# GpSimd adds the final norm's shift in place of VectorE, in the last stage of a decoder layer

## The chip, the cores and the metric

The kernel runs on one core of one Trainium2 chip. Its time is the device time in microseconds (us) of that core. Before the change it is 2271.53 us, the median of 3 runs (2271.29 to 2274.31). The engines are called by the profile's names: PE is TensorE, PEld its weight load, DVE VectorE, ACT ScalarE, POOL GpSimd, and SP the engine that issues DMAs.

## The reference

One layer of a decoder runs for 1024 prompt tokens and 8 sample tokens: attention with three key/value sets, a gated linear recurrence, a merge, a first layer norm, a mixture of 64 experts with a shared expert, and a second layer norm. What matters here is the last line:

```
def layer_norm(x, g, b):
    mu = mean(x); var = mean(square(x - mu))
    return (x - mu) * rsqrt(var + 1e-5) * g + b
...
    ffn = moe(x)                                       # routed + shared experts
    return layer_norm(DN_ALPHA * x + ffn, ln2_g, ln2_b)   # 1024 + 8 rows of 1024
```

The other place that the diff touches is the decode attention over the selected keys: a masked softmax of 8 sample tokens, whose probabilities are scaled, turned by PE and multiplied with the values.

## The kernel before

Each engine runs its own program in order; the engines meet through semaphores. A helper keeps count of them: `E.do(ins, sem)` lets an instruction raise a semaphore (its engine's own chain if none is named), `E.step(ins, sem)` does that and then waits for it on the same engine.

The order of the work is written out by hand. After the attention and the merge comes the expert stage, a loop in which PE multiplies, ACT and DVE take PSUM out, and POOL gathers and scatters rows by indirect DMA. When it is over, SP loads two sets of sums back from memory (L748, L750) into `x1tok` and `other`: nine tiles, eight of 128 tokens and one of the 8 sample tokens, 1024 columns each, float32.

The last stage ("tail") goes tile by tile, m = 0 to 8:

- PE (L1530) adds the two sets of a tile into PSUM, with the identity as weights; there are four PSUM places, so that from the fifth tile on it waits for `normed` of the tile four back. It raises `summed`.
- DVE (L2607 to L2613) waits for `summed` of tile m and takes its statistics: two BATCH_NORM_STATS2 over the halves (L2419, L2420), BATCH_NORM_AGGREGATE (L2421), adding epsilon (L2422). Then it runs `scaled_out(m - 1)` for the tile before: wait for `normed`, multiply by the scale `lnw[:, 2]` (L2601), add the shift `lnw[:, 3]` (L2602), raise `fin_done`. Then it waits for ACT's square root of tile m, takes the reciprocal (L2612) and minus the mean times it (L2613, a SCALAR_TENSOR_TENSOR of 128x1 whose two tensor inputs both lie in SBUF), and raises `mean_done`.
- ACT takes the square root (L1925) and, after `mean_done`, writes the normed tile from PSUM into `x1tok` (L1927), raising `normed`.
- SP (L753 to L755) waits for `fin_done` of each tile and writes it out. At the end it waits for all outputs.
- POOL has nothing in the tail. Its last instructions are those of the expert loop (L2708 to L2713, L2699).

In the decode attention, `dp_ready` counts the steps of DVE's probabilities: PE waits for 4, 5 and 6 before it turns pieces of them, and DVE raises it to 6 at L2215. DVE then copies the turned second half out of PSUM (L2217) and raises `dt_ev2`, for which PE waits at L1200, with `held` (POOL's copies) behind it. Later DVE raises `dp_ready` once for each block of the recurrence (L2278), and ACT waits for 6 + n at L1793.

Of the kernel before, what the change touches and what calls it, by code (L numbers as in the profile page):

```python
# [17 lines left out]
ALU = mybir.AluOpType  # L18
# [9 lines left out]
NT = SEQ // P + 1  # L28
# [161 lines left out]
def build(nc, a, o, x1_dram, y_dram):  # L190
    ctx = ExitStack()
    with ctx:
        arena = ctx.enter_context(nc.sbuf_tensor("arena", [P, 52736], F32))
        PS = ctx.enter_context(nc.psum_tensor("PS", [P, 8, 512], F32))
        names = {}

        def sem(name):
            if name not in names:
                names[name] = ctx.enter_context(nc.semaphore(name))
            return names[name]  # L200
# [4 lines left out]
        def at(off, *shape):  # L205
            n = int(np.prod(shape))
            assert off + n <= 52736, (off, shape)
            v = arena[:, off:off + n]
            if len(shape) == 2:
                v = v.rearrange("p (a b) -> p a b", a=shape[0])  # L210
            elif len(shape) == 3:
                v = v.rearrange("p (a b c) -> p a b c", a=shape[0], b=shape[1])
            return v
# [90 lines left out]
        PTb = at(TMP + 4100, NPG, 64)  # L304
# [40 lines left out]
        def quarter(x, h, j):  # L345
            return x[:, h * HT + j * QT:h * HT + (j + 1) * QT]
# [5 lines left out]
        x1tok = at(12256, NT, D)  # L352
        xr = at(21472, 2, D)
        lnw = at(25568, 4, D)
# [135 lines left out]
        def rows_of(t):  # L490
            return P if t < NT - 1 else BD
# [41 lines left out]
        def targets(i):  # L533

            u1, u0 = ucb[:, 1, 3:3 + NTOK], ucb[:, 0, 3:3 + NTOK]
            if i in (0, 2, 4):
                return u1, u0
            if i in (1, 3, 6):
                a0, b0 = {1: (1, 2), 3: (0, 1), 6: (2, 0)}[i]
                return gg[:, a0, :], gg[:, b0, :]  # L540
            if i == 5:
                return gg[:, 1, :], u1
            if i < YA:
                return mT[:, 2 * (i - YB), :], mT[:, 2 * (i - YB) + 1, :]
            if i < GX:
                return RT[:, 2 * (i - YA), :], RT[:, 2 * (i - YA) + 1, :]
            return sg[:, 0, :], sg[:, 1, :]
# [211 lines left out]
        def _(pe):  # L759
            E = Engine(pe, sem("pe_chain"), met[0], met[1:])  # L760
# [110 lines left out]
            for j in range(NT - 1):  # L871
                t = ORDER[j + 1]
# [140 lines left out]
            def own_values(slot, cols, first):  # L1013

                for b in range(BD):
                    probs = (pself[0:8, 2, :] if slot else sm_self[0:8, :])[:, col[b]:col[b] + 8]
                    ins = pv(b, probs, kvtok(8)[0:BD, cols:cols + P], first=first and b < 4)
                return ins
# [178 lines left out]
            dt_end(turn(PS[0:8, bank, 0:64], pself[0:64, 1, 0:8], 64), "own")  # L1197
            dt_taken("own")
            own_values(1, 384, False)
            pe.wait_ge(sem("dt_ev2"), 1)  # L1200
            pe.wait_ge(sem("held"), 2)
            for h4 in range(2):
                for t in range(NPG):
# [144 lines left out]
            for m in range(1, NT):  # L1348
                t = TAIL[m]
# [172 lines left out]
            for t in range(NT):  # L1522
                m, n = t, rows_of(t)
# [11 lines left out]
        def _(act):  # L1535
            E = Engine(act, sem("act_chain"), met[1], (met[0], met[2]))
            fn = nc.scalar.activation

            def copy(out, in_):
                return fn(out, in_, ACT.Copy)  # L1540
# [53 lines left out]
            for j in range(NT - 1):  # L1594
                m, t = j + 1, ORDER[j + 1]
# [112 lines left out]
            for b in range(1, BD):  # L1708
# [10 lines left out]
                if b == 6:  # L1719
                    n = ct_at["s"]  # L1720
                    act.wait_ge(sem("ct_done"), PC + n + 1)
                    E.do(copy(sm_self[0:8, :], PS[0:8, CT_BANKS[n % 3], 0:64]), sem("ct_a"))
                    n = ct_at["p"]
# [55 lines left out]
            def gelu_of(u):  # L1779

                act.wait_ge(st_cb, ADD * (u + 1))
                g = gg[:, GELU[u], :].rearrange("p h (t j c) -> p h t j c", t=2, j=2)[:, :, :, u % 2, :]
                E.do(fn(g, g, ACT.Gelu_apprx_tanh), sem("g_ev"))

            for i in range(len(PAIRS)):
                d1, d2 = targets(i)
                for j in range(2):
                    u, bank = 2 * i + j, 4 * j
                    n = AFTER.get(u - 1)
                    if n is not None:  # L1790
                        act.wait_ge(sem("r_mm"), n + 1)
                        if n:
                            act.wait_ge(sem("dp_ready"), 6 + n)  # L1793
                        E.do(fn(rr.rearrange("p (a b) -> p a b", a=4), PS[:, bank:bank + 4, 0:QT], ACT.Sigmoid, bias=vec[:, n, 37:38]), sem("r_ev"))
                        act.wait_ge(sem("i_mm"), n + 1)
                        if n:
                            act.wait_ge(sem("hs_done"), n)
                        E.do(fn(ii.rearrange("p (a b) -> p a b", a=4), PS[:, 4 - bank:8 - bank, 0:QT], ACT.Sigmoid, bias=vec[:, n, 38:39]), sem("i_ev"))
                    act.wait_ge(st_mm, PROD * u + 1)
                    if j == 0 and i in (0, 2, 4):  # L1800
                        act.wait_ge(sem("xc_done"), i + 1)
                    if j == 0 and i in (3, 5, 6):
                        act.wait_ge(sem("stg_done"), 2 if i == 3 else 5)
                    if i >= GX and u - 2 * GX >= 2:
                        act.wait_ge(sem("mg_done"), u - 2 * GX - 1)
                    E.do(copy(quarter(d1, 0, j), PS[:, bank, 0:QT]), st_ev)
                    if n is not None:
                        E.step(fn(aa, rr, ACT.Exp, scale=lam[:, 3, n:n + 1]))
                        E.do(fn(RT[:, n, :], aa, ACT.Square))
                        E.do(fn(rr, rr, ACT.Tanh, scale=lam[:, 4, n:n + 1]), sem("a_done"))  # L1810
                    act.wait_ge(st_mm, PROD * u + 2)
                    if i == 5 and j == 0:
                        act.wait_ge(sem("xc_done"), 6)
                    E.do(copy(quarter(d2, 1, j), PS[:, bank + 2, 0:QT]), st_ev)
                    act.wait_ge(st_mm, PROD * u + 4)
                    E.do(copy(quarter(d1, 1, j), PS[:, bank, 0:QT]), st_ev)
                    if n is not None:
                        act.wait_ge(sem("v_done"), n + 1)
                        E.do(fn(rr, rr, ACT.Sqrt), sem("sq_done"))
                    if u - 1 in GELU and u < 2 * YB:  # L1820
                        gelu_of(u - 1)
                    if u == 2 * YB - 1:
                        gelu_of(u)
                    if i >= GX:
                        act.wait_ge(st_cb, ADD * u + ADD)
                        both = sg.rearrange("p h (t j c) -> p h t j c", t=2, j=2)[:, :, :, j, :]
                        E.do(fn(both, both, ACT.Sigmoid), sem("sg_done"))
                if i == YB:
                    E.arrive()
                    act.wait_ge(sem("stg_T"), 1)  # L1830
                    for h in range(2):
                        E.do(copy(orows[0:20, 4 * h:4 * h + 4, :], PS[0:20, 2 + h, :].rearrange("p (k c) -> p k c", k=4)), sem("stg_ev"))
# [21 lines left out]
            for m in range(NT):  # L1854
                n = rows_of(TAIL[m])
# [65 lines left out]
            for t in range(NT):  # L1921
                m, n = t, rows_of(t)
# [8 lines left out]
        def _(dve):  # L1931
            E = Engine(dve, sem("dve_chain"), met[2], (met[0], met[1]))
            V = nc.vector
            tt, ts, stt = V.tensor_tensor, V.tensor_scalar, V.scalar_tensor_tensor
# [199 lines left out]
            for b in range(1, BD):  # L2134
# [20 lines left out]
                if b == 6:  # L2155
                    n = ct_at["s"]
                    dve.wait_ge(sem("ct_done"), PC + n + 1)
                    E.do(V.memset(sm[0:64, 5, 4:5], 0.0), sem("ct_d"))
                    n = ct_at["p"]
# [54 lines left out]
            E.step(ts(SS[0:64, 1024:2049], SS[0:64, 1024:2049], sm[0:64, 2, 4:5], None, ALU.mult), sem("dp_ready"))  # L2214
            E.step(ts(pself[0:64, 1, 0:8], const("own", 64), SS[0:64, 2048:2049], None, ALU.mult), sem("dp_ready"))  # L2215
            dve.wait_ge(sem("vec_T"), 2)
            E.do(V.tensor_copy(PTb[:, 8:16, :], PS[:, 4, :].rearrange("p (k c) -> p k c", k=8)), sem("dt_ev2"))  # L2217


            dve.wait_ge(sem("vec_ev"), 1)  # L2220
# [142 lines left out]
            for i in range(YB):  # L2363
                for j in range(2):
                    u = 2 * i + j
                    n, turns = AFTER.get(u - 1), CONV.get(u, ())
# [31 lines left out]
            for i in range(YB, len(PAIRS)):  # L2398
                if i == GX:
                    right_rest("gx")  # L2400
                for j in range(2):
# [5 lines left out]
                    if i >= GX:  # L2407
                        n = i - GX
# [40 lines left out]
            for m, t in enumerate(TAIL):  # L2449
                n = rows_of(t)  # L2450
                y, s = x1tok[0:n, t, :], st[0:n, m % 2, :]
# [50 lines left out]
            for t in range(NT):  # L2502
                n = rows_of(t)
# [24 lines left out]
            for t in range(NT):  # L2528
                n = rows_of(t)
# [17 lines left out]
            for t in range(NT):  # L2547
                n = rows_of(t)
# [48 lines left out]
            def scaled_out(t):  # L2597

                y = x1tok[0:rows_of(t), t, :]
                dve.wait_ge(sem("normed"), t + 1)  # L2600
                E.step(tt(y, y, lnw[0:rows_of(t), 2, :], ALU.mult))  # L2601
                E.do(tt(y, y, lnw[0:rows_of(t), 3, :], ALU.add), sem("fin_done"))  # L2602

            for t in range(NT):
                m, n = t, rows_of(t)
# [12 lines left out]
        def _(pool):  # L2618
            G = nc.gpsimd
# [106 lines left out]
            def spare(i, s):  # L2726
                rows_in(i + 1, s, i * 3 + 3, False)
                rows_out(i, s)
# [11 lines left out]
            for lo, hi in SPARE:  # L2740
                with pool.If(blocks > 2 * lo):
                    with pool.Fori(lo, hi) as i:
                        with pool.If(i * 2 < blocks):
                            spare(i, 0)
                            with pool.If(i * 2 + 1 < blocks):
                                spare(i, 1)


# [44 lines left out]
```

## Time and profile before

| | |
|---|---|
| time, median of 3 (lowest, highest) | 2271.53 us (2271.29, 2274.31) |
| the profiled execution's span | 2268.4 us |
| the profiled execution's own time | not listed by itself; the three runs lie 2.9 to 5.9 us over the span |
| busy share: PE, DVE, ACT, POOL | 96%, 42%, 29%, 20% |
| the tail: first matmul to the end of the span | 2217.97 to 2268.4 us |

The span runs from the first to the last instruction of the program. The page's shares are means over stages with different limits, so the tail has to be read by itself: in the views' rows a start and a duration stand first, then engine, line and operation, and in square brackets the idle time before it and what ended it.

### The profile page before, as it was taken

The page shows a single profiled execution, that of the slowest core. Times are in us where ns is not written, and L with a number is a line of the kernel's source. Part 1 is how long each engine was busy: PE and PEld are TensorE (multiplying, and loading weights), DVE is VectorE, ACT ScalarE, POOL GpSimd, SP SyncE. Part 2 cuts the span into 40 slices and gives each one's busy share as a digit, 9 for nine tenths or more (in the row PEclk, how much of TensorE's full clock was granted, in tenths as well). Part 3 has the DMA queues.
Part 4 walks back from the last instruction along what each step waited for, and adds up shares of the span by engine and source line. Part 5 has one row for each costly group of instructions (what it writes and reads, how often), then busy time and mean ns, then how long its engine had stood idle before and what let it go on. Part 6 is the DMA issues. An engine that isn't in the chain of part 4 may idle for free.

```text
span 2268.4 us, 28838 instructions
## 1 busy us (share of the span) xinstructions
PE 2182.6 (96%) x10100; PEld 1394.7 (61%) x10100; DVE 962.6 (42%) x2071; ACT 651.9 (29%) x1375; POOL 456.0 (20%) x890
## 2 busy tenths in 40 slices
PE   8998999999999999999999999999999999999985
PEld 6454665667778887888885556454544454544442
DVE  0226888754357775354444568411111111111116
ACT  3125666654425552011111220011111111111112
POOL 0002444310100000000000000144343434343430
PEclk9998999999999999999999999999999999999997
DMA  6302000053621111122213123699999999999945
GB/s 213 114 0 103 2 1 1 24 205 153 236 57 38 38 38 39 28 65 75 75 38 118 75 100 119 238 360 339 357 341 347 338 356 334 362 334 342 341 103 224
DMA packets 133214, 378.25 MB, mean 167 GB/s; under 512 B 23891, under 2 KB 81355, under 8 KB 105835
## 3 DMA queue, kind: packets, MB, share of 16 engines
q1 hardware_dynamic: 109587, 292.46, 34.5%
q0 software_dynamic: 23520, 84.36, 12.9%
q8 instruction: 69, 1.13, 0.2%
q14 instruction: 38, 0.31, 0.0%
HBM read 341.48 MB, written 58.00 MB: 176 GB/s over the span
## 4 chain that ended last, share of the span: by engine, by line
PE 84%; DVE 9%; ACT 3%; issue 2%; DMA 2%; SPq 0%; DVEq 0%; POOL 0%; ACTq 0%; POOLq 0%
PE PS L1449 20%; PE PS L1229 19%; PE PS L1460 10%; PE PS L764 8%; PE PS L877 5%; PE PS L1354 5%; PE PS L910 3%; PE PS L947 3%; PE PS L1047 2%; PE PS L812 1%; PE PS L1393 1%; PE PS L1176 1%; PE PS L1338 1%; ACT arena L1540 1%; DVE arena L2098 1%
## 5 line engine op out<-in xcount | busy, mean ns | idle before, releaser
L1229 PE MATMUL PS<-arena 128*128 128x258 f32 x2352 | 517.1, 382 | 6.3 <-DVE arena L2292 4.7
L1229 PEld LDWEIGHTS PS<-arena 128*128 128x128 f32 x2352 | 447.6, 191 | 73.9 <-DVE arena L2292 5.1
L1540 ACT ACTIVATE arena<-PS 128x512 f32<-128x512 f32 (+9 forms) x602 | 276.2, 471 | 724.3 <-PE PS L764 401.9
L1449 PE MATMUL PS<-arena 128*128 128x512 f32 x1040 | 457.2, 592 | 0.8 <-ACT arena L1540 0.8
L764 PEld LDWEIGHTS PS<-arena 128*128 128x128 f32 (+3 forms) x1950 | 234.0, 158 | 186.6 <-issue 127.2
L1449 PEld LDWEIGHTS PS<-arena 128*128 128x128 f32 x1040 | 192.9, 190 | 218.6 <-issue 217.6
L764 PE MATMUL PS<-arena 128*128 128x128 f32 (+3 forms) x1950 | 285.7, 278 | 30.1 <-DVE arena L2074 8.1
L1460 PE MATMUL PS<-arena 128*128 128x512 f32 x520 | 239.2, 593 | 0.5 <-ACT arena L1540 0.5
L2564 DVE TENSOR_TENSOR arena<-PS,arena 128x256 f32<-128x256 f32 x65 | 27.6, 425 | 432.3 <-ACT arena L1882 432.3
L1460 PEld LDWEIGHTS PS<-arena 128*128 128x128 f32 x520 | 94.0, 191 | 93.9 <-issue 93.3
L2677 POOL MEMSET arena<- 128x2 f32 x1 | 0.1, 100 | 746.4 <-PE PS L1354 746.4
L2639 POOL TENSOR_SCALAR arena<-arena 128x384 f32<-128x384 f32 (+3 forms) x192 | 103.6, 565 | 141.3 <-DVE arena L2051 95.8
L2571 DVE TENSOR_SCALAR arena<-PS,arena 128x512 f32<-128x512 f32 x65 | 48.8, 750 | 188.9 <-PE PS L1460 188.9
L1635 ACT ACTIVATE arena<-PS,arena 128x384 f32<-128x384 f32 (+3 forms) x192 | 104.7, 550 | 48.9 <-DVE arena L2022 43.5
L1882 ACT ACTIVATE arena<-PS 128x256 f32<-128x256 f32 x65 | 25.0, 384 | 319.5 <-PE PS L1449 319.5
L877 PE MATMUL PS<-arena 128*128 128x512 f32 x256 | 116.6, 596 | 0.0
L1354 PE MATMUL PS<-arena 128*128 128x512 f32 x256 | 113.1, 595 | 0.0
L2713 POOL DMA_INDIRECT expert_rows<-arena,dsts x65 | 104.3, 1605 | 36.2 <-issue 36.2
L910 PE MATMUL PS<-arena 64*128 64x384 f32 (+3 forms) x384 | 86.3, 529 | 5.9 <-ACT arena L1635 5.1
L2022 DVE TENSOR_REDUCE arena<-PS 128x2 f32<-128x768 f32 (+3 forms) x96 | 85.5, 891 | 11.7 <-PE PS L910 9.0
L1890 ACT ACTIVATE arena<-PS,arena 128x512 f32<-128x512 f32 x65 | 44.7, 688 | 147.3 <-PE PS L1460 147.3
L1354 PEld LDWEIGHTS PS<-arena 128*128 128x128 f32 x256 | 47.4, 190 | 54.1 <-issue 54.0
(337 smaller groups left out, 2212.6 us busy)
## 6 DMA issues: line engine op xcount, KB each, us to landing
arena<-in_w_exp_gate SPq DMA_DIRECT2D x65, 1024.0 KB, 7.4
arena<-in_w_exp_up SPq DMA_DIRECT2D x65, 1024.0 KB, 10.4
arena<-in_w_exp_down SPq DMA_DIRECT2D x65, 1024.0 KB, 9.4
arena<-in_w_in SPq DMA_DIRECT2D x34, 512.0 KB, 4.7
arena<-in_x_prompt SPq DMA_DIRECT2D x16, 512.0 KB, 5.6
expert_rows<-arena SPq DMA_DIRECT2D x16, 512.0 KB
arena<-expert_rows SPq DMA_DIRECT2D x6, 1024.0 KB, 12.2
arena<-in_w_in SPq DMA_DIRECT2D x16, 256.0 KB, 8.0
```

The lines of the kernel that those rows point to most:

```text
L764: return nc.tensor.transpose(out, in_, ident[0:n, 0:n])
L877: ins = mm(PS[:, 2 * (j % 2) + c, :], xT[:, k, t * P:(t + 1) * P], wtb[:, k, c * 512:(c + 1) * 512], start=k == 0, stop=k == KT - 1)
L910: ins = mm(PS[:, b + g, 0:n], qrT[GP[g], u["j"], q], kvT[GP[g], col, c0:c0 + n], start=True, stop=True)
L1229: ins = mm(PS[:, bank, 0:QT], lhs[:, l0 + k, :], right[:, r0 + k, c0:c0 + QT], start=first and k == 0, stop=k == kh - 1, skip_group_check= ...
L1354: ins = mm(PS[:, 2 * (m % 2) + c, :], mT[:, k, t * P:(t + 1) * P], wout[:, k, c * 512:(c + 1) * 512], start=k == 0, stop=k == KT - 1)
L1449: ins = mm(PS[:, 2 + s, :].rearrange("p (h n) -> p h n", h=2), xgT[:, s, k, :], up_w[w][:, :, k, :], start=k == 0, stop=k == KT - 1)
L1460: ins = mm(PS[:, 4 + 2 * s + c, :], hT[:, s, k, :], down_w[w][:, k, c * 512:(c + 1) * 512], start=k == 0, stop=k == 1)
L1540: return fn(out, in_, ACT.Copy)
L1635: E.do(fn(probs(u)[:, g, :, :], PS[:, b + g, 0:u["n"] * P].rearrange("p (t c) -> p t c", c=P), ACT.Exp, bias=negm[:, h, kd, u["chunk"], g: ...
L2022: E.do(V.tensor_reduce(negm[:, h, kd, u["chunk"], :], S, AX, ALU.max, negate=True), mx_done)
L2639: ins = G.tensor_scalar(v, v, coef[:, h, kd, u["chunk"], g:g + 1], 1.0, ALU.mult, ALU.mult)
L2713: G.indirect_dma_start(out=y_rows, out_offset=bass.IndirectOffsetOnAxis(ap=dsts[:, s:s + 1], axis=0), in_=ysb[:, s, :], in_offset=None, bo ...
```

## The change

Tile by tile in the tail, DVE only multiplies and raises a new semaphore `scaled`; POOL waits for it and adds the shift, and raises `fin_done`. POOL's nine adds stand at the end of its program, behind the expert loop. To have a semaphore for that, `dt_ev2` goes: the copy at L2217 raises `dp_ready` to 7 instead, PE waits for 7 of it, and ACT's later waits go up by one.

```
             own_values(1, 384, False)
-            pe.wait_ge(sem("dt_ev2"), 1)
+            pe.wait_ge(sem("dp_ready"), 7)
...
                         if n:
-                            act.wait_ge(sem("dp_ready"), 6 + n)
+                            act.wait_ge(sem("dp_ready"), 7 + n)
...
-            E.do(V.tensor_copy(PTb[:, 8:16, :], PS[:, 4, :].rearrange("p (k c) -> p k c", k=8)), sem("dt_ev2"))
+            E.do(V.tensor_copy(PTb[:, 8:16, :], PS[:, 4, :].rearrange("p (k c) -> p k c", k=8)), sem("dp_ready"))
...
                 y = x1tok[0:rows_of(t), t, :]
                 dve.wait_ge(sem("normed"), t + 1)
-                E.step(tt(y, y, lnw[0:rows_of(t), 2, :], ALU.mult))
-                E.do(tt(y, y, lnw[0:rows_of(t), 3, :], ALU.add), sem("fin_done"))
+                E.do(tt(y, y, lnw[0:rows_of(t), 2, :], ALU.mult), sem("scaled"))
...
                             with pool.If(i * 2 + 1 < blocks):
                                 spare(i, 1)
+            for t in range(NT):
+                y = x1tok[0:rows_of(t), t, :]
+                pool.wait_ge(sem("scaled"), t + 1)
+                G.tensor_tensor(y, y, lnw[0:rows_of(t), 3, :], ALU.add).then_inc(sem("fin_done"), 1)
```

## Rows read from the trace of the kernel before

**Rows 1.** Chain that ended last, tail: start us, us, what (xcount).

```profile
2217.97 9.00 PE PS L1530 x16
2226.98 0.02 issue
2227.00 0.70 DVE arena L2419
...
2230.02 1.23 DVE arena L2602
...
2262.45 1.21 ACT arena L1927
```

**Rows 2.** Busy time by windows, the tail's three stretches, us.

```profile
2227.00:2251.10 24.10, 24.09 (x56) 9.34 (x54) 23.13 (x45) 7.47 (x12) 0.00 (x0) 1.00 0.63 254
2251.10:2268.40 17.30, 0.00 (x0) 0.00 (x0) 13.33 (x22) 4.01 (x5) 0.00 (x0) 0.54 0.23 93
```

**Rows 3.** Timeline of the tail, one tile and the last (start us, us, instruction).

```profile
2228.76 1.23 DVE L2601 TENSOR_TENSOR arena<-arena 128x1024 f32<-128x1024 f32 x1
2230.02 1.23 DVE L2602 TENSOR_TENSOR arena<-arena 128x1024 f32<-128x1024 f32 x1
2231.16 0.16 DVE L2612 RECIPROCAL arena<-arena 128x1 f32<-128x1 f32 x1
2231.36 0.16 DVE L2613 SCALAR_TENSOR_TENSOR arena<-arena 128x1 f32<-128x1 f32 x1
2231.43 0.69 DVE L2419 BATCH_NORM_STATS2 arena<-PS 128x6 f32<-128x512 f32 x1
2233.19 1.23 DVE L2601 TENSOR_TENSOR arena<-arena 128x1024 f32<-128x1024 f32 x1
...
2257.97 0.68 DVE L2419 BATCH_NORM_STATS2 arena<-PS 8x6 f32<-8x512 f32 x1
2259.69 1.23 DVE L2601 TENSOR_TENSOR arena<-arena 128x1024 f32<-128x1024 f32 x1
2262.27 0.15 DVE L2613 SCALAR_TENSOR_TENSOR arena<-arena 8x1 f32<-8x1 f32 x1
2263.68 1.21 DVE L2601 TENSOR_TENSOR arena<-arena 8x1024 f32<-8x1024 f32 x1 [1.26 <-ACT arena L1927]
2264.93 1.21 DVE L2602 TENSOR_TENSOR arena<-arena 8x1024 f32<-8x1024 f32 x1
2266.17 0.30 SPq L755 DMA_DIRECT2D out_y_s<-arena  x1
```

**Rows 4.** POOL's groups by form: count | busy us, mean ns | idle before.

```profile
L2634 POOL TENSOR_TENSOR arena<-arena 128x504 f32<-128x504 f32 x8 | 8.3, 1033 | 20.1 <-DVE arena L2039 20.1
L2665 POOL COPY arena<-arena 128x1024 f32<-128x1024 f32 x1 | 1.0, 1037 | 0.8 <-PE PS L1058 0.8
L2709 POOL TENSOR_TENSOR dsts<-tokall,izero 128x1 int32<-128x1 int32 x65 | 12.2, 188 | 0.0
```

**Rows 5.** Timelines of DVE and of POOL, decode attention, 589 to 597 us.

```profile
589.69 1.29 DVE L2190 TENSOR_TENSOR arena<-arena 64x1089 f32<-64x1089 f32 x1
592.33 1.29 DVE L2192 TENSOR_TENSOR arena<-arena 64x1089 f32<-64x1089 f32 x1
593.65 2.86 DVE L2193 TENSOR_TENSOR arena<-arena 64x1089 f32<-64x1089 f32 x1
...
592.63 2.73 POOL L2672 COPY arena<-arena 128x2048 f32<-128x2048 f32 x1 [6.71 <-PE PS L987]
```

**Rows 6.** The same two timelines, prompt attention: 8-element operations near POOL's.

```profile
234.56 0.28 DVE L2039 TENSOR_TENSOR arena<-arena 128x8 f32<-128x8 f32 x1
...
234.23 0.59 POOL L2639 TENSOR_SCALAR arena<-arena 128x384 f32<-128x384 f32 x1
...
277.55 0.19 DVE L2037 TENSOR_SCALAR arena<-arena 128x8 f32<-128x8 f32 x1
...
277.58 0.61 POOL L2639 TENSOR_SCALAR arena<-arena 128x384 f32<-128x384 f32 x1
...
358.69 0.62 DVE L2037 TENSOR_SCALAR arena<-arena 128x8 f32<-128x8 f32 x1
...
358.69 0.59 POOL L2639 TENSOR_SCALAR arena<-arena 128x384 f32<-128x384 f32 x1
```

**Rows 7.** The same, where a POOL add-like operation waits for DVE from idle.

```profile
384.77 0.17 DVE L2039 TENSOR_TENSOR arena<-arena 128x8 f32<-128x8 f32 x1
...
385.03 1.03 POOL L2634 TENSOR_TENSOR arena<-arena 128x504 f32<-128x504 f32 x1 [0.55 <-DVE arena L2039]
...
409.75 0.17 DVE L2039 TENSOR_TENSOR arena<-arena 128x8 f32<-128x8 f32 x1
...
410.00 1.03 POOL L2634 TENSOR_TENSOR arena<-arena 128x504 f32<-128x504 f32 x1 [0.55 <-DVE arena L2039]
```

**Rows 8.** Line L2217, decode attention: who waited for it.

```profile
L2217 DVE COPY arena<-PS x1: 691/691/691, 632.5 to 632.5; 128x512 f32<-128x512 f32 x1
...
  PEld PS L987: 0.2, 1
```

## The prediction

> **What bounds the kernel now.** The page first: PE is busy 96% of the span, but that is a mean over stages, and the change stands in the last 50 us. So I read the chain of waits for the tail. Up to 2227.0 us it runs on PE's matmuls; from there to the end it runs on DVE, through its statistics, L2601 and L2602, tile after tile, with one step of ACT (L1927) for the last tile [rows 1]. The windows say the same: from 2227.0 to 2251.1 DVE is busy 23.13 of 24.10 us, and PE 24.09, because both run at full tilt; after 2251.1 PE has nothing left, and DVE goes on alone for 15 us [rows 2]. PE is the faster of the two: its 56 matmuls are seven tiles, 24.1 / 7 = 3.44 us a tile. DVE's period is from one L2601 to the next, 2233.19 - 2228.76 = 4.43 us [rows 3]. So DVE bounds the tail, and POOL has no instruction in it [rows 2]. In DVE's period, multiply and add take 1.26 us each from start to start, and the rest, 1.91, is the two small operations and the statistics.
>
> **The change part by part.**
>
> *Joined semaphore.* `dp_ready` is raised by DVE in program order; its seventh step is now the very copy that raised `dt_ev2`, so PE is released at the same moment (it waited 0.2 us there) [rows 8], and ACT's 7 + n names the same recurrence block as 6 + n did. No instruction is added or removed. Bound from both sides 0, as the waits end on the same instructions. Cost: 0.
>
> *DVE's add goes.* Nine TENSOR_TENSOR of 128x1024 (the last 8x1024). Each removes 1.26 us from DVE's period, eight times on the chain, and one more after the last multiply. `E.step` of the multiply becomes `E.do`: the wait on itself goes, but the reciprocal behind it stood behind an `E.do` before too, so it starts 0.09 us ahead of the large operation's end as now (2231.16 against 2230.02 + 1.23 = 2231.25) [rows 3]. 0.
>
> *POOL's add comes.* No row has POOL adding 1024 float32 columns. The nearest is its multiply of 128x504, two tensor inputs, 1.033 us; in proportion, 1.033 x 1024 / 504 = 2.10 us. From below: with POOL's one-column operation of 0.188 us as the fixed part, 0.188 + 1023 x (1.033 - 0.188) / 503 = 1.91 us. From above: two COPY of 1024 columns, one for each input, and the fixed part, 2 x 1.037 + 0.188 = 2.26 us [rows 4]. I take 2.10, the 504 row being the only two-input one of any size. The Trainium skill ("GPSIMD Engine Reference", section 3.1's table of measured numbers) gives 4497 ns for an add of 2048 columns, an estimate of 2.3 us for 1024; no row here shows that size, and the sum below would be 2279.6 by it. POOL starts 0.09 us after the DVE instruction that releases it ends (384.77 + 0.17 = 384.94, start 385.03; 409.75 + 0.17 = 409.92, start 410.00) [rows 7]. The output's DMA waits for `fin_done` as before; after the last it is 2.3 us to the end (2266.14 to 2268.4) [rows 3], unchanged.
>
> *What the add does to DVE.* This decides. In the trace, a DVE operation with two SBUF inputs doesn't run beside a POOL operation that reads SBUF. DVE's L2192 and L2190 take 1.29 us; the same form, L2193, issued at 593.65 while POOL's COPY runs until 592.63 + 2.73 = 595.36, takes 2.86 and ends at 596.51, 1.15 us after POOL. And that COPY, issued 0.3 us after L2192, takes 2.73 us where two of 1024 columns would be 2.07 [rows 4, 5]. It holds for tiny operations: L2039, 8 columns, takes 0.28 in place of 0.17 us and ends 0.02 us after POOL's (234.84 against 234.82) [rows 6, 7]. So whoever asks first keeps the other out for its whole instruction.
> Now L2613: two SBUF inputs, 128x1, and it comes right behind the multiply, 0.11 us after the end of the large operation (2231.36 - 2231.25) [rows 3]. POOL's add is released by the same multiply and starts 0.09 us after its end. POOL is ahead by 0.02 us. How close can it be? Two rows tell: a DVE operation that starts in the same 0.01 us as a POOL operation (both 358.69) waits for the whole of it, 0.62 us; one that starts 0.03 us before POOL's (277.55 against 277.58) goes through in 0.19, and POOL's takes 0.61 in place of 0.59 [rows 6]. So at 0.02 behind, L2613 waits until POOL's add is over, and with it everything that follows on DVE (the next tile's statistics) and ACT's L1927, which waits for `mean_done`.
> The Trainium skill ("SBUF — State Buffer", section "Who interferes with whom") speaks against the change: DVE and GpSimd share a read port, held for a whole instruction by whichever issued first, and a DVE operation with two SBUF inputs wants it. The rows above show the same; by it the sum is the one below, and by a view that small operations pass freely it is the first rival's.
>
> *The sum.* L2613 ended 0.27 us after the large operation (2231.36 + 0.16 - 2231.25). Now it ends 0.09 + 2.10 + 0.01 = 2.20 after it, 1.93 later. Against the 1.26 saved, each period is 0.67 us longer, 5.10 us. L2613 is held eight times (tiles 1 to 8): 8 x 0.67 = 5.4 us. After the last multiply, POOL's 0.09 + 2.10 = 2.19 stands for DVE's 0.04 + 1.21 = 1.25: 0.9 us more. Together +6.3 us. The multiply of the next tile never meets an add, since the add is over before the statistics run. PE waits for its PSUM places by a us at most: tile 4 is normed at about 2228.76 + 3 x 5.10 + 1.23 + 2.20 + 1.2 = 2248.7 us, for PE's last tile, which starts about 3.5 before 2251.1, and which DVE doesn't need before 2267. The profiled execution's 2268.4 becomes 2274.7; the median of the runs lies 3.1 us above the span, and what lies around the span doesn't change, so 2271.5 + 6.3 = 2277.8 us. With 1.91 for the add it is 8 x 0.48 + 0.75 = +4.6 (2276.1), with 2.26 it is 8 x 0.83 + 1.1 = +7.7 (2279.3).
>
> **The rivals.**
>
> *First, the other side: L2613 gets in ahead of the add.* It decides on 0.02 us: if POOL takes its inputs a little after its recorded start, or DVE asks at once, L2613 passes, POOL waits some 0.15 us, and DVE's period is 4.43 - 1.26 = 3.17, under PE's 3.44. Then PE bounds the tail: its last sum is ready at 2251.1 as now [rows 2], and the last tile's statistics start there and not at 2257.97, 6.9 us sooner. The last multiply would start at 2251.1 + (2263.68 - 2257.97) - 1.26 = 2255.55, finds the add of the tile before (over at about 2256.3), ends at about 2257.5, and the last add at 2259.7, against 2266.14: -6.4 us, 2265.1 us. For it: the margin is at the edge of what the timeline resolves, and the two rows on order are of POOL operations in a row, not from idle. Against it: both rows put the border on POOL's side. It would also come out this way (2264.4) if so small a read weren't held at all, against which the 8-column rows speak.
>
> *Second: the order changes from tile to tile.* With a margin of 0.02 us, some of the eight are held and others not. A half each gives 4 x 5.10 + 4 x 3.3 = 33.6 us for eight periods against 35.4, so -1.8 + 0.9 = -0.9, about 2270.6 us. For it: the margin; against it: POOL's start behind DVE's end is within 0.01 us in the two cases that stand in the rows.
>
> *Third: POOL becomes the bound.* If L2613 passes but the add is long (2.26), multiply, add and the two handovers make 1.23 + 0.2 + 2.26 = 3.7 us a tile, over PE's 3.44: +1.8 us on the first rival, 2267 us.
>
> **How the numbers follow.** The forecast (every L2613 held) has a chance of 0.68, the first rival 0.19, the second 0.08, the third 0.05. A measurement of this kernel can tell about 0.2% (4.5 us) from no change: the borders are 2267.0 and 2276.1. The forecast's own range is 2275 to 2281 us, from the add's bounds and some spread of the runs; about 0.08 of its 0.68 falls under 2276.1. Slower 0.60. Within: 0.08, the second rival, and a part of the third, 0.17. Faster: the first rival and the rest of the third, 0.23. No range holds 8 in 10 without the first rival, so it reaches from 2264.5 to 2281.
>
> **What would show it.** In the changed kernel's timeline: POOL's 128x1024 TENSOR_TENSOR at about 2.1 us, starting 0.09 us after L2601's end; L2613 at about 2.1 us in place of 0.16, ending with POOL's; L2601 still 1.23; DVE's period 5.1 us. The chain would go through POOL's adds and L2613, and the last multiply start near 2269 us. If L2613 stays at 0.16 us and the last statistics start at 2251.1, right behind PE, the forecast is wrong and the first rival has it; durations that differ between tiles would be the second. A shift before 2217 us would mean that the joined semaphore wasn't free.

## The result: slower, and by more than forecast

The changed kernel takes 2283.56 us, the median of 4 runs (2281.61 to 2285.78), against 2272.77 us for the kernel before in 4 runs (2271.29 to 2274.31). The ratio is 1.0051, with a 95% interval of 1.0039 to 1.0063, or 9 to 14 us of loss, 11.6 at its middle. The forecast was 2277.8 us, +6.3, in a range up to 2281: the side was right, the size not.

### Profile after: where the time is

The timeline of the changed kernel's VectorE in the tail, one tile; a start and a duration stand first. It answers to [rows 3], with L2613 now called L2612.

```profile
2231.86 1.22 DVE L2601 TENSOR_TENSOR arena<-arena 128x1024 f32<-128x1024 f32 x1
2233.01 0.16 DVE L2611 RECIPROCAL arena<-arena 128x1 f32<-128x1 f32 x1
2233.20 2.33 DVE L2612 SCALAR_TENSOR_TENSOR arena<-arena 128x1 f32<-128x1 f32 x1
2235.45 0.68 DVE L2419 BATCH_NORM_STATS2 arena<-PS 128x6 f32<-128x512 f32 x1
...
2237.20 1.22 DVE L2601 TENSOR_TENSOR arena<-arena 128x1024 f32<-128x1024 f32 x1
...
2269.16 1.23 DVE L2601 TENSOR_TENSOR arena<-arena 128x1024 f32<-128x1024 f32 x1
```

And GpSimd's timeline there, the first, the eighth and the ninth of its adds.

```profile
2233.17 2.34 POOL L2749 TENSOR_TENSOR arena<-arena 128x1024 f32<-128x1024 f32 x1 [20.45 <-DVE arena L2601]
...
2270.46 2.34 POOL L2749 TENSOR_TENSOR arena<-arena 128x1024 f32<-128x1024 f32 x1 [2.96 <-DVE arena L2601]
2275.36 2.33 POOL L2749 TENSOR_TENSOR arena<-arena 8x1024 f32<-8x1024 f32 x1 [2.56 <-DVE arena L2601]
```

SyncE's timeline there, its last output.

```profile
2277.72 0.30 SPq L755 DMA_DIRECT2D out_y_s<-arena  x1
```

The multiply ends at 2231.86 + 1.22 = 2233.08; GpSimd's add starts 0.09 us later; the tiny operation starts at 2233.20, 0.03 behind the add, and ends at 2235.53, 0.02 after it (2233.17 + 2.34 = 2235.51). One column takes 2.33 us. The line's own view shows that eight of nine are so, the least being the first tile's, which meets no add (operation, count, then duration least/median/most in ns):

```profile
L2612 DVE SCALAR_TENSOR_TENSOR arena<-arena x9: 159/2327/2335, 2228.9 to 2270.5; 128x1 f32<-128x1 f32 x8, 8x1 f32<-8x1 f32 x1
```

VectorE's period is 2237.20 - 2231.86 = 5.34 us, against 4.43 [rows 3]. VectorE waits for no other engine between its operations until its last multiply, so the 2.33 us of the held one lie in every period.

A second term is at the very end, behind the last instruction of work. From GpSimd's last add (2275.36 + 2.33 = 2277.69) to the end of the span at 2283.1 it is 5.4 us; before, 2.3 us lay behind VectorE's last add [rows 3]. The view of the program's closing line, L192, of both kernels shows why. First the kernel before.

```profile
L192 POOLq DRAIN  x1: 6441/6441/6441, 2210.5 to 2210.5; - x1
...
L192 SPq DRAIN  x1: 12/12/12, 2268.1 to 2268.1; - x1
```

Then the changed one.

```profile
L192 POOLq DRAIN  x1: 7571/7571/7571, 2275.3 to 2275.3; - x1
...
L192 SPq DRAIN  x1: 13/13/13, 2279.7 to 2279.7; - x1
L192 SPq EVENT_SEMAPHORE  x1: 17/17/17, 2283.1 to 2283.1; - x1
```

GpSimd's program closes with a DRAIN, an instruction of the program's end and not of the kernel's work, that is recorded from where its last instruction is issued (2275.3) to 2282.9, which is 5.2 us after that instruction ended. Before, it ran from 2210.5 to 2216.9 while TensorE waited for DMAs. Now it stands behind the last add. The output itself has landed by SyncE's own DRAIN at 2279.7, and the last 3.4 us wait for GpSimd alone. The view of SyncE's waits has the 3.4 us, but puts them down to the wrong engine (TensorE's DRAIN was long over); before, that row read 0.2.

```profile
SPq L192 <- PEq L192: 3.4, 1, 3.4
SPq L192 <- DMA out_y_s<-arena: 1.5, 1, 1.5
```

To add it up, I count from where both tails are set by TensorE: the start of the second tile's statistics, 2227.00 before [rows 1] and 2230.10 after. To the end of the span that is 41.4 and 53.0 us, 11.6 more. From the first large multiply to the eighth, 37.30 against 30.93 us: +6.4. From there to the end of the last add, 8.53 against 6.45: +2.1. Behind it, 5.41 against 2.26: +3.15. The sum of the three is the middle of the measured loss. The 3 us by which this profile's tail starts later come on top in this one execution; such starts move between executions (below).

### The profile page after: what moved, and what is told of

It reads as the page before. It is cut to its first block, busy times and chain, and to the rows that moved or that the text cites. A ratio compares the mean times of both kernels' runs of the same rounds, so it can differ in the third digit from the quotient of the medians.

```text
span 2283.1 us, 28838 instructions
## 1 busy us (share of the span) xinstructions
PE 2185.2 (96%) x10100; PEld 1396.2 (61%) x10100; DVE 968.8 (42%) x2062; ACT 651.2 (29%) x1375; POOL 476.1 (21%) x899
## 4 chain that ended last, share of the span: by engine, by line
PE 84%; DVE 9%; ACT 3%; issue 2%; DMA 2%; POOL 0%; POOLq 0%; SPq 0%; DVEq 0%; ACTq 0%
PE PS L1449 20%; PE PS L1229 19%; PE PS L1460 10%; PE PS L764 8%; PE PS L877 5%; PE PS L1354 5%; PE PS L910 3%; PE PS L947 3%; PE PS L1047 2%; PE PS L812 1%; PE PS L1393 1%; PE PS L1176 1%; PE PS L1338 1%; ACT arena L1540 1%; DVE arena L2612 1%
## 5 line engine op out<-in xcount | busy, mean ns | idle before, releaser
L1229 PEld LDWEIGHTS PS<-arena 128*128 128x128 f32 x2352 | 446.7, 190 | 73.9 <-DVE arena L2292 5.1
L1449 PEld LDWEIGHTS PS<-arena 128*128 128x128 f32 x1040 | 192.9, 190 | 218.6 <-issue 217.6
L1460 PEld LDWEIGHTS PS<-arena 128*128 128x128 f32 x520 | 94.0, 191 | 93.9 <-issue 93.3
L1882 ACT ACTIVATE arena<-PS 128x256 f32<-128x256 f32 x65 | 24.9, 383 | 319.6 <-PE PS L1449 319.6
L2707 POOL TENSOR_TENSOR pause<-izero 128x1 int32<-128x1 int32 x65 | 12.6, 194 | 333.8 <-DVE arena L2571 333.0
```

What stands on the lines that cost most here:

```text
L1229: ins = mm(PS[:, bank, 0:QT], lhs[:, l0 + k, :], right[:, r0 + k, c0:c0 + QT], start=first and k == 0, stop=k == kh - 1, skip_group_check= ...
L1449: ins = mm(PS[:, 2 + s, :].rearrange("p (h n) -> p h n", h=2), xgT[:, s, k, :], up_w[w][:, :, k, :], start=k == 0, stop=k == KT - 1)
L1460: ins = mm(PS[:, 4 + 2 * s + c, :], hT[:, s, k, :], down_w[w][:, k, c * 512:(c + 1) * 512], start=k == 0, stop=k == 1)
```

## The experiments

The times before are those of the runs on the same chips: 2272.33 us (27 runs, for the first four kernels) and 2272.1 us (24 runs, for the other four). The tail is compared by the same stretch, second statistics to end of span: 41.4 us before, 53.0 changed.

### The joined semaphore alone

```
-            pe.wait_ge(sem("dt_ev2"), 1)
+            pe.wait_ge(sem("dp_ready"), 7)
...                                  # and 7 + n, and the copy raising dp_ready; the adds stay on VectorE
```

> The kernel before with the joined semaphore alone; the tail is as before. Theory (the loss is all in the tail and behind it): no change, within 1.5 us of the kernel before, last statistics at the same distance from PE's first tail matmul. Rival (the join delays something, as the tail of the changed kernel's profile began 2.8 us later): about +2.8 us, and the tail starts that much later.

2274.25 us, ratio 1.0005 (0.9996 to 1.0014). Its tail is 2273.3 - 2231.94 = 41.4 us, as before, yet it starts 4.9 us later than in the profile before, later even than in the changed kernel's. The late start alone doesn't speak for the join: in the traces of two kernels below that keep `dt_ev2` the second statistics start at 2229.63 and 2230.84, against 2227.00 before, and of those that have the join one starts them at 2228.00. So without any change ahead of it the tail moves by 3.8 us, more than the rival's 2.8. TensorE waits 0.2 us for the copy that raises the joined semaphore, as before. The ratio finds no cost, but its interval reaches +3.2 us, so it doesn't by itself shut out the rival's 2.8.

### VectorE adds the last tile

```
-            for t in range(NT):                      # GpSimd's loop
+            for t in range(NT - 1):
...
+                else:                                # VectorE, last tile
+                    E.step(tt(y, y, lnw[0:rows_of(t), 2, :], ALU.mult))
+                    dve.wait_ge(sem("fin_done"), t)
+                    E.do(tt(y, y, lnw[0:rows_of(t), 3, :], ALU.add), sem("fin_done"))
```

> The changed kernel, but VectorE adds the last tile's shift itself, so that GpSimd's last add is that of the eighth tile. Theory (GpSimd's program needs 5.2 us after its last instruction before the execution can end): its last add ends at the place of 2272.8 in the changed kernel's trace, its closing at 2278.0, VectorE's last add at 2276.5 and its output 2.3 us later, 2278.8: 4.3 us less than the changed kernel, about +7 us against the kernel before. Rival (the closing is no term; only the last add counts): the last add ends 1.1 us earlier and the time falls by 1.1 us, about +10. The held SCALAR_TENSOR_TENSOR stays at 2.33 us for both.

2280.56 us, ratio 1.0038 (1.0024 to 1.0052), against 1.0051: by the middles 3 us less, by intervals that overlap. The traces are sharper: the tail is 2278.4 - 2229.77 = 48.6 us, 4.4 under the changed kernel's, where 4.3 were expected and the rival had 1.1. GpSimd's DRAIN now ends at 2277.7, half a microsecond before SyncE's:

```profile
L192 POOLq DRAIN  x1: 7581/7581/7581, 2270.1 to 2270.1; - x1
...
L192 SPq DRAIN  x1: 13/13/13, 2278.2 to 2278.2; - x1
```

### One SBUF tensor input in place of two

```
-                E.do(stt(s[:, 0:1], s[:, 12:13], -1.0, s[:, 15:16], ALU.mult, ALU.mult), sem("mean_done"))
+                E.do(ts(s[:, 0:1], s[:, 12:13], s[:, 15:16], -1.0, ALU.mult, ALU.mult), sem("mean_done"))
```

> The changed kernel, but the tiny operation before mean_done is a TENSOR_SCALAR with a pointer scalar: one SBUF tensor input and not two. Theory (it is held only because its second SBUF input needs the port that GpSimd reads through): it takes 0.16 us, the large multiply and the add then take turns, 1.23 + 2.34 + 0.1 = 3.67 us a tile, the last add ends at about 2261.6 of a trace that starts its tail as the kernel before, and with GpSimd's closing of 5.2 us the time is about 1.5 us below the kernel before (4.5 below without the closing). Rival (any small VectorE operation behind GpSimd's start is held, or it waits for GpSimd in another way): no change from the changed kernel, about +11 us.

2270.89 us, ratio 0.9994 (0.9985 to 1.0003): 13 us by the ratios under the changed kernel, from one tiny instruction. The same two numbers are multiplied, but the second comes as a pointer scalar (one value for each partition) and not as a tensor, and it isn't held. It runs while GpSimd adds, as the two engines' timelines show:

```profile
2231.80 0.21 DVE L2612 TENSOR_SCALAR arena<-arena 128x1 f32<-128x1 f32 x1
...
2231.77 2.35 POOL L2749 TENSOR_TENSOR arena<-arena 128x1024 f32<-128x1024 f32 x1 [20.46 <-DVE arena L2601]
```

The view of the tiny line:

```profile
L2612 DVE TENSOR_SCALAR arena<-arena x9: 201/214/215, 2227.5 to 2256.6; 128x1 f32<-128x1 f32 x8, 8x1 f32<-8x1 f32 x1
```

The view of the large multiply's line:

```profile
L2601 DVE TENSOR_TENSOR arena<-arena x9: 1224/1471/1928, 2230.5 to 2258.1; 128x1024 f32<-128x1024 f32 x8, 8x1024 f32<-8x1024 f32 x1
```

The waiting has moved, as expected, to the large multiply (two SBUF inputs), which now meets the add of the tile before and takes up to 1.93 us; the turns of multiply and add settle at 3.51 us a tile (GpSimd's adds start at 2249.33 and 2252.85), against TensorE's 3.44. The tail is 39.2 us, 2.2 under the kernel before, and at its end stands GpSimd's closing of 5.2 us: the last add ends at 2262.41, the output is out by 2264.4, the closing is over at 2267.6 and the span ends at 2267.9.

### One column at the end, by GpSimd

```
+            pool.wait_ge(sem("fin_done"), NT)       # kernel before, end of GpSimd's program
+            G.tensor_tensor(pause[:, 0:1], izero[:, 0:1], izero[:, 0:1], ALU.add).then_inc(sem("ix0"), 1)
```

> The kernel before, and GpSimd adds one column of integers after the last tile's add of VectorE. Theory (closing of 5.2 us after GpSimd's last instruction): it ends at 2266.4 of the trace before, closing at 2271.6: +3.4 us. Rival (the closing runs beside the last work, or starts at a fixed place): 0, as the output lands 2.3 us after VectorE's last add in any case.

2276.6 us, ratio 1.0017 (1.0008 to 1.0026): +3.9 us for one instruction of 0.19 us. GpSimd's timeline:

```profile
2268.86 0.19 POOL L2748 TENSOR_TENSOR pause<-izero 128x1 int32<-128x1 int32 x1 [55.97 <-DVE arena L2602]
```

GpSimd's closing, from the view of line L192:

```profile
L192 POOLq DRAIN  x1: 5436/5436/5436, 2268.8 to 2268.8; - x1
```

The add ends at 2269.05, the DRAIN at 2274.25, again 5.2 us later, though the instruction before it is a twelfth as long as the changed kernel's last add. The tail is 2274.5 - 2229.63 = 44.9 us, 3.5 over the kernel before, where 3.4 were expected.

### The order turned round

```
-                if m:                                # ahead of the tiny operations of tile m
-                    scaled_out(m - 1)
...
                 E.do(stt(s[:, 0:1], s[:, 12:13], -1.0, s[:, 15:16], ALU.mult, ALU.mult), sem("mean_done"))
+                if m:
+                    scaled_out(m - 1)
```

> The changed kernel with the two-input form kept, but VectorE's large multiply of tile m - 1 placed behind the tiny operations of tile m. Theory (whoever asks first holds the port for a whole instruction): the tiny operation meets only the end of the add of two tiles back, is held 0.1 to 0.2 us in place of 2.2, the period falls from 5.33 to about 3.75 us, and the time is about 11 us under the changed kernel, the kernel before within 2 us (the closing of 5.2 us still stands at the end). Rival (the two-input form is slow whenever GpSimd adds at all): the operation stays over 1 us, and the time within 4 us of the changed kernel.

2272.51 us, ratio 1.0006 (0.9995 to 1.0017): 10 us by the ratios under the changed kernel. The tail is 2268.4 - 2228.00 = 40.4 us. The two-input form is kept, and it is held for 0.1 us only:

```profile
L2610 DVE SCALAR_TENSOR_TENSOR arena<-arena x9: 158/263/297, 2226.8 to 2255.6; 128x1 f32<-128x1 f32 x8, 8x1 f32<-8x1 f32 x1
```

So the form alone isn't slow; what it meets in time decides. The period is 3.57 us (I had said 3.75).

### VectorE alone, its add behind the tiny operations

```
+            def shifted(t):                          # kernel before; called behind mean_done of tile t + 1
+                y = x1tok[0:rows_of(t), t, :]
+                E.do(tt(y, y, lnw[0:rows_of(t), 3, :], ALU.add), sem("fin_done"))
```

> The kernel before, GpSimd not used: VectorE's add of tile m - 1 placed behind the tiny operations of tile m, beside ScalarE. Theory: VectorE bounds the tail and its work is the same, so only the last tile gains, about 1.2 us, as ScalarE's last 1.2 us then lie beside an add. Rival (the order is worth what the best version gains, and GpSimd nothing): -4 us or more.

2271.93 us, ratio 0.9994 (0.9985 to 1.0003). In the trace the tail is 39.3 us, 2.1 shorter and not 1.2: the period fell from 4.42 to 4.30 too. The ratio can't tell it from no change, and its interval stays clear of the best version's (below, 0.9956 to 0.9979).

### A broadcast second input

```
+                v = y.rearrange("p (a b) -> p a b", a=16)
+                G.tensor_tensor(v, v, lnw[0:rows_of(t), 3, 0:16].unsqueeze(2).broadcast_to([rows_of(t), 16, 64]), ALU.add)
```

> The changed kernel, GpSimd's second input a broadcast of 16 values over 64 columns each (the shift itself is left out), as in the 128x504 row from which 2.10 us was taken. Theory (that row is cheaper for its broadcast input): the add takes about 1.9 to 2.1 us in place of 2.34, and the tiny operation shrinks with it. Rival (the rate does not depend on it and grows with the columns in another way): 2.34 us stays.

This kernel leaves the shift itself out, and there is one run of it, so only its trace is used. The add of 1024 columns takes 1.90 us when its second input holds 16 values, each read 64 times, and the held operation shrinks with it, to 1.89. The tail is 2281.2 - 2232.06 = 49.1 us, 3.9 under the changed kernel's: nine times the 0.44 us. The view of the add's line:

```profile
L2750 POOL TENSOR_TENSOR arena<-arena x9: 1890/1899/1900, 2235.1 to 2273.8; 128x1024 f32<-128x1024 f32 x8, 8x1024 f32<-8x1024 f32 x1
```

And of the tiny operation's:

```profile
L2612 DVE SCALAR_TENSOR_TENSOR arena<-arena x9: 158/1887/1894, 2230.9 to 2269.4; 128x1 f32<-128x1 f32 x8, 8x1 f32<-8x1 f32 x1
```

### The best version

```
+                E.do(ts(s[:, 0:1], s[:, 12:13], s[:, 15:16], -1.0, ALU.mult, ALU.mult), sem("mean_done"))
+                if m == NT - 1:
+                    shifted(m - 1)                   # VectorE adds the eighth tile beside ScalarE
...
+            for t in range(NT - 2):                  # GpSimd adds seven of nine
```

> TENSOR_SCALAR form of the tiny operation; GpSimd adds tiles 0 to 6, VectorE the last two, the eighth tile's add behind the last mean_done, beside ScalarE's last tile. Theory (held operation, add of 2.34 us and closing of 5.2 us are all that the change costs): PE sets the pace until its last sum at 2251.1 of the trace before, statistics and multiply to 2254.1, tiny operations to 2254.4, VectorE's add beside ScalarE's 1.2 us, last multiply and add 2.5 us, output 2.3 us: about 2262.5 in place of 2268.4, -6 us against the kernel before; GpSimd's closing ends by 2260 and is hidden. Rival (something else in GpSimd's part of the tail costs): not under the kernel before by more than 2 us.

2265.41 us, ratio 0.9968 (0.9956 to 0.9979) to the kernel before: 7.3 us less (5 to 10), and 19 by the ratios under the changed kernel. The tail is 2264.4 - 2230.64 = 33.8 us against 41.4. GpSimd's last add starts at 2254.76 and its closing is over by 2262.3, before the last output has landed. VectorE's last stretch:

```profile
2256.64 1.54 DVE L2601 TENSOR_TENSOR arena<-arena 128x1024 f32<-128x1024 f32 x1
2258.11 0.14 DVE L2616 RECIPROCAL arena<-arena 8x1 f32<-8x1 f32 x1
2258.28 0.20 DVE L2617 TENSOR_SCALAR arena<-arena 8x1 f32<-8x1 f32 x1
2258.41 1.20 DVE L2606 TENSOR_TENSOR arena<-arena 128x1024 f32<-128x1024 f32 x1
2259.75 1.21 DVE L2601 TENSOR_TENSOR arena<-arena 8x1024 f32<-8x1024 f32 x1
2260.99 1.21 DVE L2606 TENSOR_TENSOR arena<-arena 8x1024 f32<-8x1024 f32 x1
```

The add at 2258.41 is over at 2259.61, before ScalarE's last tile lets the multiply at 2259.75 start, so it costs nothing. Three things are changed at once here: the form, the place of the eighth tile's add, and who makes the last two adds. VectorE alone, with its adds moved, got 2.1 of the 7.6 us in its own trace, so not all of them are GpSimd's.

## Why the prediction was right in kind and wrong in size

- *What bounds the tail.* Right: VectorE before and after; with the hold taken away, the pace falls to 3.51 us, next to TensorE's 3.44.
- *Joined semaphore, 0.* Not contradicted: 1.0005, with an interval of -0.9 to +3.2 us, and a tail of unchanged length. A cost of a us or two ahead of the tail isn't shut out.
- *The tiny operation is held.* Right, in all eight tiles that meet an add, with the start 0.03 us behind GpSimd's (0.02 was read). The two experiments that let it through, by its form and by its place, took away 13 and 10 us. The Trainium skill ("SBUF — State Buffer", section "Who interferes with whom") gives the rule behind it: a VectorE instruction with two SBUF inputs contends with a GpSimd instruction that reads SBUF, and one with a single SBUF input doesn't, unless it runs in one of VectorE's two-port modes. The traces agree for this pair, 2.33 us for the two-input form and 0.21 for the other. The two-input one doesn't always pay all of it: with the order turned round it met only the end of GpSimd's add and took 0.1 us longer.
- *How close it is, by L2037 [rows 6].* The two rows from which the race was judged show a TENSOR_SCALAR of eight columns with one SBUF input and a constant, `ts(v, v, 1e-30, None, ALU.max)`. The prediction took them for L2613's case, which has two tensor inputs and one column. One of them was held for all of GpSimd's all the same, 0.62 us. So that a one-input operation passes is shown here for one column only, and no run tells why L2037 was held.
- *POOL's add, "I take 2.10, the 504 row being the only two-input one of any size".* Mis-sized: 2.34 us, outside the bounds of 1.91 and 2.26 too. The row of 128x504 [rows 4] has a broadcast second input, and the run with a broadcast of 1024 columns took 1.90, what that row gave from below. The reference row's operands were not those of the new operation. It costs 8 x 0.24 on the held operation and 0.24 on the last add, 2.2 us. The Trainium skill's figure ("GPSIMD Engine Reference", section 3.1), from which 2.3 was estimated, was the better one here; its row is a two-input add of float32 as well.
- *"The output's DMA waits for `fin_done` as before; after the last it is 2.3 us to the end (2266.14 to 2268.4) [rows 3], unchanged."* This step failed. It is 5.4 us, since the end waits for GpSimd's closing too, 5.2 us behind its last instruction. I had counted what is queued behind the add on GpSimd's engine as nothing, as no instruction of the kernel is; the closing was in the trace before, in the stretch after 2210.5, where it was covered. One column of integers at the end shows the cost by itself, +3.9 us.
- *Readings that were off and cost nothing.* TensorE waited 1.9 us for its PSUM places, not "a us at most", and VectorE was to need the last sum at 2257.97 + 7 x 0.67 = 2262.7 by the prediction's own periods, not 2267; in the changed trace the sum was ready some 10 us before VectorE took it. The 3.1 us from span to time mix two executions, since every listed run lies 1.8 to 2.3 us over its own span; the sum works with differences, so it isn't touched.

The sum with both put right: 6.3 + 2.2 + 3.15 = 11.6 us, the middle of the measured ratio. Without the closing it would have been 8.5, inside the range.

The rivals: the first (the tiny operation gets in ahead) is what two experiments make of the kernel. Its multiplies do meet the adds, as it said, but it lacked the closing: it gave -6.4 us where the tail of the one-input version is 2.2 shorter. Of the 4.2 between, 3.2 are the closing (5.5 us lie behind the last add, in place of 2.3), 0.8 are TensorE's last sum, which was ready 24.9 us after the second statistics and not 24.1, and 0.2 the longer add. The second, an order that changes from tile to tile, didn't occur. The third, the add as the bound, is what the one-input version shows, at 3.51 us a tile where 3.7 were reckoned: a multiply that was held ends 1.08 us after the add, not 1.23.

## What to carry to other kernels

Before you move a pass to GpSimd, look at every VectorE instruction that will run beside it, the one-column ones first: one with two SBUF tensor inputs waits for the whole of GpSimd's, and for one column a pointer scalar in place of the second tensor took that away. A one-input operation of eight columns was held too [rows 6], so look at the trace for each. Let GpSimd finish some 6 us before the end of the program. And take a duration from a row only if its operands are of the same kind, broadcast ones included.

## What the runs showed that I had not expected

- GpSimd's closing DRAIN lasts 5.2 us after its last instruction, be that an add of 2.33 us, one column of 0.19 us, or (before) a DMA issue. What it does in that time no view shows.
- A broadcast second input makes GpSimd's two-input add of 1024 columns 1.90 us in place of 2.34, and the sample tile's add over 8 partitions takes as long as one over 128, 2.33.
- The start of the tail differs by up to 5 us between executions (second statistics at 2227.00 to 2232.06 us in ten traces; 2227.00 to 2230.84 in the three with no change ahead of it), more than most effects here. Part of it stands long before: the copy at L2217 started between 632.2 and 635.8. A stretch counted within each trace, from the second statistics to the end, was 41.4 us both before and with the joined semaphore. By these two traces it resolves effects in the tail that the ratios (0.1% or 2 us to either side) leave open.
